# A two-layer decoder step: a shorter last layer, attention in pairs over both key groups, six banks for the merge and the feed-forward, loops written out, and the second norm's halves made straight from x

## The reference

```
h = rmsnorm(x) * norm1_g
q_m,k_m,v_m,i,f,o, glu_a,glu_b, q_a,k_a,v_a, g_pre = split(h @ w_in)
x = x + (g_a * mlstm(..) @ w_mlstm_out + g_b * conv(..) @ w_conv_out + g_c * attn(..) @ w_attn_out) @ w_out
h2 = rmsnorm(x) * norm2_g
x = x + (silu(causal_conv3(h2 @ w_ffn_gate)) * (h2 @ w_ffn_up)) @ w_ffn_down
```

## Time and profile before

| | |
|---|---|
| median of 3 runs | 1176.4 us (1175.46 to 1188.33) |
| the profiled execution | 1183.7 us |
| its span, first to last instruction | 1181.9 us |
| mean granted TensorE clock | 0.951 of full speed |
| PE busy | 1097.0 us (93%) in 7854 matmuls |
| DVE busy | 800.1 us (68%) |
| ACT busy | 537.5 us (45%) |
| POOL busy | 129.5 us (11%) |
| DMA | 168.49 MB, mean 143 GB/s |

### The profile page before, as it was taken

One profiled execution on the slowest core, in us unless ns is written; L12 is line 12 of the kernel. 1 busy time (PEld: TensorE's weight loads), 2 busy tenths in 40 slices (PEclk: granted clock), 3 DMA queues, 4 the chain that ended last, 5 costly groups with the idle time before them and its releaser, 6 DMA issues.

```text
span 1181.9 us, 22212 instructions
## 1 busy us (share of the span) xinstructions
PE 1097.0 (93%) x7854; PEld 1031.5 (87%) x7854; DVE 800.1 (68%) x1453; ACT 537.5 (45%) x942; POOL 129.5 (11%) x109
## 2 busy tenths in 40 slices
PE   5999999889888999999969999998898979999997
PEld 3989879778788999999969898896797979999996
DVE  4586976655687677775356788776458767777753
ACT  4535543224643455553344445431273435555532
POOL 0020000222100122110000200022130002122000
PEclk9999999888899999999979999998798989999999
DMA  9654446162445575555576454362453537655551
GB/s 246 150 129 114 125 107 158 53 165 74 145 131 143 143 221 173 163 167 168 154 173 148 112 141 106 98 155 72 125 151 109 159 101 214 188 164 171 162 173 50
DMA packets 318529, 168.49 MB, mean 143 GB/s; under 512 B 25174, under 2 KB 317334, under 8 KB 318218
## 3 DMA queue, kind: packets, MB, share of 16 engines
q1 hardware_dynamic: 318266, 165.83, 51.4%
q10 hardware_dynamic: 144, 1.14, 0.2%
HBM read 160.45 MB, written 9.71 MB: 144 GB/s over the span
## 4 chain that ended last, share of the span: by engine, by line
PE 65%; DVE 13%; issue 13%; ACT 3%; DMA 2%; POOL 1%; DVEq 1%; SPq 0%; ACTq 0%; POOLq 0%
PE ps_tile L824 19%; PE ps_tile L825 18%; PE ps_tile L826 18%; DVE w_lo L1617 4%; DVE uc L1712 2%; DMA w_raw<-in_w_in 2%; ACT w_hi L1194 2%; POOL gate_buf L1513 1%; PE work L951 1%; PE work L921 1%; PE work L1040 1%; PE work L1042 1%; DVE c_head L1910 1%; PE work L1047 1%; DVE prod L1666 1%
## 5 line engine op out<-in xcount | busy, mean ns | idle before, releaser
L1617 DVE TENSOR_TENSOR w_lo<-w_raw,w_hi 128x1024 fp32r<-128x1024 f32 (+1 forms) x288 | 343.4, 1196 | 141.2 <-ACT w_hi L1194 136.7
L1194 ACT ACTIVATE w_hi<-w_raw 128x1024 fp32r<-128x1024 f32 (+1 forms) x288 | 294.7, 1027 | 121.1 <-DMA w_raw<-in_w_ffn_down 61.1
L824 PE MATMUL ps_tile<-h_hi,w_hi 128*128 128x280 f32 (+1 forms) x1008 | 308.4, 306 | 14.4 <-DVE h_lo L1627 9.3
L825 PE MATMUL ps_tile<-h_lo,w_hi 128*128 128x280 f32 (+1 forms) x1008 | 300.3, 298 | 0.0
L826 PE MATMUL ps_tile<-h_hi,w_lo 128*128 128x280 f32 (+1 forms) x1008 | 299.1, 297 | 0.0
L824 PE MATMUL ps_tile<-xg_hi,w_hi 128*128 128x280 f32 x704 | 210.9, 300 | 13.0 <-DVE x L1668 10.4
L824 PEld LDWEIGHTS ps_tile<-h_hi,w_hi 128*128 128x128 f32 (+1 forms) x1008 | 195.0, 193 | 20.6 <-DVE h_lo L1627 9.5
L825 PE MATMUL ps_tile<-xg_lo,w_hi 128*128 128x280 f32 x704 | 207.4, 295 | 0.0
L826 PE MATMUL ps_tile<-xg_hi,w_lo 128*128 128x280 f32 x704 | 207.2, 294 | 0.0
L825 PEld LDWEIGHTS ps_tile<-h_lo,w_hi 128*128 128x128 f32 (+1 forms) x1008 | 194.9, 193 | 1.2
L826 PEld LDWEIGHTS ps_tile<-h_hi,w_lo 128*128 128x128 f32 (+1 forms) x1008 | 194.2, 193 | 0.6
(11 more groups left out here) (307 smaller groups left out, 1438.0 us busy)
## 6 DMA issues: line engine op xcount, KB each, us to landing
w_raw<-in_w_in SPq DMA_DIRECT2D x98, 512.0 KB, 4.1
w_raw<-in_w_ffn_gate SPq DMA_DIRECT2D x44, 512.0 KB, 3.9
w_raw<-in_w_ffn_up SPq DMA_DIRECT2D x44, 512.0 KB, 3.9
w_raw<-in_w_ffn_down SPq DMA_DIRECT2D x32, 512.0 KB, 3.8
w_raw<-in_w_out SPq DMA_DIRECT2D x16, 512.0 KB, 3.8
w_raw<-in_w_ffn_down SPq DMA_DIRECT2D x14, 384.0 KB, 3.5
w_raw<-in_w_in SPq DMA_DIRECT2D x20, 256.0 KB, 3.4
c_head<-in_state_mlstm_c SPq DMA_DIRECT2D x8, 512.0 KB, 4.8
```

The lines of the kernel that those rows point to most:

```text
L824: mm(out, hi[:, k, :], a_hi[:, k0 + k, :], start=first, stop=False, skip_group_check=True)
L825: mm(out, hi[:, k, :], a_lo[:, k0 + k, :], start=False, stop=False, skip_group_check=True)
L1194: go(h, r, ACT.Copy).then_inc(w_hi_ready, 1)
L1617: tt(lo, r, h.bitcast(F32), ALU.subtract).then_inc(w_split[n % SLOTS], 1)
```

## The change

1. **Shorter last layer.** In layer 1 the pieces `o`, `g`, `yc`, `yb`, `ya`, `out`, `gate`, `up` and `down`, and all that takes and splits them, leave out token columns 0 to 13: f = 14, 266 columns in place of 280. Two meta columns stay for the 3-tap convolution. The final norm too begins at column 14.
2. **Attention in pairs.** A unit is (block, pair of heads) over both key groups. Score and value products alternate between partitions 0 to 63 and 64 to 127 (scores) or output partitions 0 to 63 and 64 to 127 (values), into banks `work0` and `work1` for the scores. The value products are half as wide and twice as many.
3. **Six banks from `ya` on.** `tile_banks = ps_tile + work[2:5]`; `glub` to `yb` keep three. `ya0` waits until the mLSTM result has left the `work` banks.
4. **Loops written out.** `for l in range(DEPTH)` in place of `Fori` on all five engines; every wait value is a constant.
5. **No scaling of the gate on POOL.** `up` takes the silu as it is; `ffn_rms_inv` is applied once more behind the contraction, to each of the 8 `down` tiles, by one more VectorE instruction before the add to x.
6. **Second norm straight from x.** The VectorE product into `h_full` (L1671) is gone. ScalarE makes `xg_hi` from x with the `norm2` vector as its scale; VectorE makes `xg_lo` as x times `norm2` minus `xg_hi` in one three-operand instruction.

The diff, cut to its core (in the same way every `take`, split and silu of the named kinds gets `f:T` in place of `:`):

```
+KEPT_FROM = N_META - (FFN_CONV_W - 1)
+NOT_KEPT = ("o", "g", "yc", "yb", "ya", "out", "gate", "up", "down")
+def first_token(l, kind):
+    return KEPT_FROM if l == DEPTH - 1 and kind in NOT_KEPT else 0
...
+WIDE_FROM = TILE_NO["ya", 0]
+for _k in TILES:
+    _t = TILE_NO[_k]
+    BANK[_k] = _t % 3 if _t < WIDE_FROM else (_t - WIDE_FROM + 3) % 6
+    BEFORE[_k] = _last.get(BANK[_k])
+    _last[BANK[_k]] = _k
...
+        tile_banks = ps_tile + work[2:5]
...
-            with nc.tensor.Fori(0, DEPTH) as l:
+            for l in range(DEPTH):
...
+                            old = BEFORE[tile]
+                            if tile == ("ya", 0):
+                                pe.wait_ge(hm_ready, value("hm_ready", l, 4))
+                            if opens and old is not None:
...
-                        mm(out, hi[:, k, :], a_hi[:, k0 + k, :], start=first, stop=False, skip_group_check=True)
+                        mm(out, hi[:, k, :], a_hi[:, k0 + k, f:T], start=first, stop=False, skip_group_check=True)
...
-                    for j in range(R_A):
-                        bank, c = divmod(j, per_bank)
-                        m = mm(work[bank][0:nq, c * nk:(c + 1) * nk], qa_t[d, j, q0:q0 + nq], ka_t[d, k0:k0 + nk],
-                               start=True, stop=True)
+                    for j in range(2):
+                        for g, d in enumerate(GROUP_ROWS):
+                            m = mm(work[g][0:nq, j * nk:(j + 1) * nk], qa_t[d, 2 * pair + j, q0:q0 + nq], ka_t[d, k0:k0 + nk],
+                                   start=True, stop=True)
...
-                        m = mm(work[4][d, 0:R_A * nq], va_rows[0:n, (k0 + c) // P, d], probs_t[0:n, u % 2, i * 512:i * 512 + R_A * nq],
-                               start=(i == 0), stop=(i == len(chunks) - 1))
+                        for g, d in enumerate(GROUP_ROWS):
+                            m = mm(work[4][d, 2 * pair * nq:2 * (pair + 1) * nq], va_rows[0:n, (k0 + c) // P, d],
+                                   probs_t[0:n, u % 2, i * 512 + 2 * g * nq:i * 512 + 2 * (g + 1) * nq],
+                                   start=(i == 0), stop=(i == len(chunks) - 1), skip_group_check=True)
...
-                    act.wait_ge(h_ready, value("h_ready", l, KD + c + 1))
-                    go(xg_hi[:, c, :], h_full[:, c, :], ACT.Copy).then_inc(h_hi_ready, 1)
+                    act.wait_ge(took_dve, value("took_dve", l, DVE_NO["out", c] + 1))
+                    go(xg_hi[:, c, f:T], x[:, c, f:T], ACT.Copy, scale=vcol("norm2", c)).then_inc(h_hi_ready, 1)
...
-                    tt(gate_buf[:, t % 4, :], gate_buf[:, t % 4, :], ffn_rms_inv[:, :], ALU.mult).then_inc(gate_scaled, 1)
...
-                    tt(xg_lo[:, c, :], h_full[:, c, :], xg_hi[:, c, :].bitcast(F32), ALU.subtract).then_inc(h_lo_ready, 1)
+                    stt(xg_lo[:, c, f:T], x[:, c, f:T], vcol("norm2", c), xg_hi[:, c, f:T].bitcast(F32), ALU.mult, ALU.subtract).then_inc(h_lo_ready, 1)
...
-                        tt(x[:, t, :], x[:, t, :], src, ALU.add).then_inc(took_dve, 1)
+                        if kind == "down":
+                            tt(gate_buf[:, t % 2, f:T], src, ffn_rms_inv[:, f:T], ALU.mult).then_inc(down_scaled, 1)
+                            dve.wait_ge(down_scaled, value("down_scaled", l, t + 1))
+                            src = gate_buf[:, t % 2, f:T]
+                        tt(x[:, t, f:T], x[:, t, f:T], src, ALU.add).then_inc(took_dve, 1)
                         dve.wait_ge(took_dve, value("took_dve", l, DVE_NO[tile] + 1))
-                        if kind == "out":
-                            ts(h_full[:, t, :], x[:, t, :], vcol("norm2", t), None, ALU.mult).then_inc(h_ready, 1)
-                            if t >= 1:
-                                second_norm_lo(t - 1)
+                        if kind == "out" and t >= 1:
+                            second_norm_lo(t - 1)
```

More of the change, by code:

```diff
@@ L199 @@
 GROUPS = [STEP["glub", 0], STEP["out", 0], STEP["gate", 0]]
-UNITS = [(blk, g) for blk in range(3) for g in range(2)]
+UNITS = [(blk, pair) for blk in range(3) for pair in range(2)]
 CONV_FROM, CONV_TO = 8, 51
@@ L546, in units_of @@
             nk = q0 + nq - k0
-            return blk, g, q0, nq, k0, nk, (4 if nk == P else 2)
+            return blk, pair, q0, nq, k0, nk
+        GROUP_ROWS = [slice(g * DH_A, (g + 1) * DH_A) for g in range(KV_A)]
         def key_chunks(nk):
@@ L790, in project @@
                             cols = slice(0, 8) if kind == "if" else slice(j * P, (j + 1) * P)
-                            out = bank[0:8, 0:T] if kind == "if" else bank[:, 0:T]
+                            out = bank[0:8, 0:T] if kind == "if" else bank[:, first_token(l, kind):T]
                             if len(pieces) == 1:
@@ L1189, in _ @@
             act.dma_start(const[:, 2 * P:CONST_COLS], consts[:, 2 * P:CONST_COLS]).then_inc(tables_in, 16)
-            with nc.scalar.Fori(0, DEPTH) as l:
+            for l in range(DEPTH):
                 def split_hi(n):
@@ L1598, in square @@
                 done = SQ_STEPS * (k - 1)
-                dst = squares[:, 1 if c == 0 else 0, :]
+                f = first_token(l, "out")
+                dst = squares[:, 1 if c == 0 else 0, f:T]
                 if c == 0:
@@ L1603, in square, with inverse_root @@
                     dve.wait_ge(squared, value("squared", l, done + 2 * c - 1))
-                tt(dst, x[:, c, :], x[:, c, :], ALU.mult).then_inc(squared, 1)
+                tt(dst, x[:, c, f:T], x[:, c, f:T], ALU.mult).then_inc(squared, 1)
                 if 0 < c < KD - 1:
                     dve.wait_ge(squared, value("squared", l, done + 2 * c))
-                    tt(squares[:, 1, :], squares[:, 1, :], squares[:, 0, :], ALU.add).then_inc(squared, 1)
-            def inverse_root(w, root, inverse):
+                    tt(squares[:, 1, f:T], squares[:, 1, f:T], squares[:, 0, f:T], ALU.add).then_inc(squared, 1)
+            def inverse_root(w, root, inverse, f):
                 dve.wait_ge(rms_ready, w)
-                dve.reciprocal(inverse[:, :], root[:, :]).then_inc(rms_inv_ready, 1)
-            with nc.vector.Fori(0, DEPTH) as l:
+                dve.reciprocal(inverse[:, f:T], root[:, f:T]).then_inc(rms_inv_ready, 1)
+            for l in range(DEPTH):
                 def split_lo(n):
@@ L1645, in take @@
                         return
-                    bank = ps_tile[TILE_NO[tile] % 3]
-                    src = bank[:, 0:T]
+                    bank = tile_banks[BANK[tile]]
+                    f = first_token(l, kind)
+                    src = bank[:, f:T]
                     tile_ready(dve, l, tile)
```

162 lines of the change are left out of this document (81 added, 81 removed).

## The result

The changed kernel took 1138.3 us (median of 4 runs, 1137.0 to 1146.4), the kernel before 1179.8 beside it: a ratio of 0.965 (95% interval 0.958 to 0.973). Two more sets of six gave 0.9645 (0.9615 to 0.9676) and 0.9669 (0.9635 to 0.9703). The forecast was 1143, a ratio of 0.972. Part of its closeness is luck: it stood on a median of 1176.4 from three runs, and larger sets of the same kernel (13, 11 and 11 runs) gave 1180.5, 1183.8 and 1180.8. Taken as savings, 33.4 us were forecast and 39 to 42 came.

The account below looks back on a forecast made before the run. TensorE was taken as the bound in `gate`/`up`, `down` and attention, VectorE at the merge's end and in `out`. Seven terms summed to 33.4 us saved: 1183.7 to 1150.3 profiled, median 1143 from 1176.4; range 1131 to 1158.

Parts of the forecast that it names:

- 1 width: Layer 1 matmuls from `o` to `down`: 14 columns fewer save 5.8 ns each, 12.6 us in all.
- 2 attention: Attention scores and values: records alternating between partition halves overlap, five slots in place of eight, saving 6.6 us.
- 3 banks at the merge: Merge: with six banks the `out` group starts 2.0 us earlier per layer, saving 4.0 us.
- 4 norm off VectorE: `out` tiles: one VectorE instruction fewer saves 0.22 us a step, 3.0 us in all.
- 5 `gate`/`up`: `gate` and `up`: six banks and no POOL remove TensorE's waits for a bank, saving 4.8 us.
- 6 loops: Between the layers: written-out loops let VectorE and TensorE go on at once, saving 3.3 us.
- 7 `down`: `down`: one more VectorE instruction per tile, only the last not hidden, losing 0.9 us over two layers.
- A: Rival: layer 1's pitch stays 128.6 ns at 266 columns, so the width gives nothing: 1156 us, chance 0.12.
- D: Rival: layer 1 products starting at column 14 stream badly, 234 ns each: slower, 1443 us, chance 0.03.
- B: Rival: pairing attention records gives nothing: 1150 us; chance 0.13 together with E.
- E: Rival: the two key groups' attention products come out one behind the other: B's time, chance 0.13 together with B.
- C: Rival: the clock stays up in the `gate` group, 7 us more saved: 1136 us, chance 0.10.

Follow-up runs that it names:

- e2: The changed kernel with all 280 columns in layer 1 again: 1153.5 us, ratio 0.9767 to the kernel before.
- e1: The kernel before with only its loops written out: 1172.7 us against 1180.5, ratio 0.9933.
- e5: The changed kernel with three banks throughout in place of six from `ya` on: 1147.6 us in one run.
- e7: The changed kernel with the second norm's product put back on VectorE: 1145.5 us, beside 1143.7 for the changed kernel.
- e6: The changed kernel with the `gate` scaling back on POOL and the additional `down` instruction gone: 1140.1 us in one run.
- e4: The changed kernel with all attention records of one key group issued before the other's, not alternating: 1149.8 us in one run.
- e3: The changed kernel with layer 1's eight `down` tiles made over ever fewer columns, 266 down to 154: 1135.6 us in one run.
- e9: The changed kernel with the `out` tiles' squares made on ScalarE, VectorE only adding them: 1135.8 us, ratio 0.9597.
- e8: The changed kernel with the `out` tiles' squares and their sums on POOL instead of VectorE: 1143.9 us, ratio 0.9659.

## Why the prediction was right, step by step

| term | predicted, us | measured, us | by |
|---|---|---|---|
| 1 width | 12.6 | 9.6 at equal clock; 12 to 14, wide interval, over all | e2 |
| 2 attention | 6.6 | 5.8 (3.3 and 2.6), 0.4 of it the width's | e1, changed |
| 3 banks at the merge | 4.0 | 5.1, of it 1.5 by the clock | e5 |
| 4 norm off VectorE | 3.0 | 3.1 | e7 |
| 5 `gate`/`up` | 4.8 | 2.3, and 3.6 that written-out loops give too | e1, e5, e6 |
| 6 loops | 3.3 | 7.9 (4.7 to 11.1), the 3.6 among them | e1 |
| 7 `down` | -0.9 | -0.95 | e6 |

**Term 6 was mis-sized, and it is the main miss.** The turn came as forecast: 3.3 less 0.5, 2.8, against 2.95 measured. But I wrote "the register work before waits goes too; I count it at nothing". It was not nothing: it made the chain that frees the banks some 0.24 us longer, and that was enough to make TensorE wait in each `gate`/`up` stretch, 1.8 us a layer. Perhaps the 2.5 us before `vm0` of layer 1 belong to it too.

**Term 5 was right in mechanism and near in size, but its gain is shared with term 6.** I gave the 2.9 us that TensorE lost in that window to banks and POOL, and the rows of the kernel before bear this out: the `gate` pieces start as soon as the product behind POOL has freed their bank. From `up1` to `down` layer 0 took 129.68 us before and takes 126.69 now, 3.0 less. What I did not see is how small the margin was. Of the 3.0 the loops alone give 1.8, with POOL and three banks in place. The other 1.2 lie in `up1` to `gate3`: 10.57 us in e1 and 9.40 after, 9.38 with POOL and six banks, 9.71 with three banks and no POOL, so either edit nearly suffices. VectorE's 33.2 us of waiting for POOL were never the price: they are the same in e1, where TensorE loses nothing in `gate3` to `down`.

**Term 1 was right in mechanism.** 5.2 ns a product, not 5.8, and not A's zero. The floor that I read from the one-column records (122 ns) was too high: it is 112. Of the 1.8 us that I had put on `o` and the first `g` e2 shows 0.8. And with POOL in the path, half of what `gate` and `up` gave would not have come (e6); the sum had the terms as independent. **Term 2** held within its ends. But my picture of records that have to alternate in the program was needless, by e4. **Terms 3, 4 and 7** were sized by one row each and came within about 1 us; that term 3 got more than its 4.0 is the clock's doing, which the term did not have.

**Rivals.** A and D are refuted by the pitch (123.6 ns from column 14 on, nothing near D's 234 at full clock, and e3's other starting columns stream at full pace), B and E by 1.14 us in place of 1.99 and by the 5.8 us of the stage. C did not happen: a stand of 3.80 us still came with a fall of the clock, one of 1.64 (e9) did not.

The start of the first products says nothing: it lies between 24.8 and 26.7 us over all kernels, and moves from run to run of one. With what two terms share counted once, the terms measured one by one add up to some 32 us, and to 37 with the largest figure for the width; the whole came to 39 to 42. The rest isn't settled. The excess of layer 0 over its 9 us is 1.8 in `gate` and `up`, 1.2 at the merge, and 4.4 in the conv and mLSTM stretches, which I had not counted on. There the clock falls in some runs and not in others: from `g9` to `ya` layer 0 took 135.6 us in the kernel before, and 130.3 to 135.1 over the twelve other profiles. So one profile of the kernel before can't tell how much of the rest these stretches gave.

## What to carry to other kernels

Idle time of an engine is no price until the bound engine is seen to wait for it, and what decides is the margin: the same 33 us of VectorE on POOL cost TensorE 1.8 us a layer when the bank came free 0.05 us before it was needed, nothing with 0.25 us to spare (e1), and 2.3 us once the products were narrower (e6). So two edits can share one gain, or one can need the other, and terms taken from one trace don't simply add. A loop kept in registers costs more than its turn, and the cheapest way to know is to write it out in the old kernel and time that alone. When an edit seems to change a stage by a few us, first lay the granted clock of the two beside each other, and compare only pieces at the same clock.

## What the runs showed of the hardware that I had not expected

- The pitch of products that each bring their own 128 x 128 weights has a floor of 112 ns, reached at 234 columns (e3). Probably the load sets it.
- Score matmuls on the two halves of the partitions ran as pairs although the program issued one half behind the other: eight records in 1.14 us in either order (e4). Whether the engine or an earlier step pairs them isn't shown.
- Beside POOL a VectorE instruction with two SBUF inputs can take nearly double its time (0.50 to 0.97 us, e8), or keep it while POOL's takes longer (e6); one with an input in PSUM kept its 0.67 us (changed kernel).
- A loop kept in registers lengthened a chain through three engines by 0.24 us in 8.8, and so cost TensorE 1.8 us in 119 where it waited for the bank at that chain's end (kernel before, e1).
- A stand of 2.7 us before the `out` group came with a clock of 0.84 behind it in one layer and of 1.00 in the other (e5): its length alone doesn't decide.
